# The low halves behind the first fused norm moved forward, the second variance behind the second fused norm moved back, and single idle products between the statistics products

## The reference, cut to what matters

```
def modulate(x, shift, scale):
    return layer_norm(x) * (1 + scale) + shift

def post_norm(x, y, gate, g, b):
    return layer_norm(ALPHA * x + gate * y) * g + b
...
        x = post_norm(x, mix_lat, g1, ln1_g[l], ln1_b[l])
        ffn_lat = conv_ffn(modulate(x, sh2, sc2), ffn_w_up[l], ffn_conv_w[l], ffn_conv_b[l], ffn_w_down[l], True)
        x = post_norm(x, ffn_lat, g2, ln2_g[l], ln2_b[l])
```

```
def hybrid_layer(h, p_i, cos, sin, g_mix, w_in, g_cq, w_q_up, w_iq_up, g_qn, g_kn, g_ik,
...
    xn = rms_norm(h, g_mix)
    proj = xn @ w_in
```

## Time and profile before

| | |
|---|---|
| Median of 3 runs | 2062.41 us (2062.07 to 2062.96) |
| The profiled execution's own time | 2063.26 us |
| Its span in the profile | 2061.5 us |
| TensorE busy | 2012.5 us, 98% |
| VectorE, GpSimd and ScalarE busy | 55%, 44%, 42% |
| p1, from the last sum to the first product that rests on it | 308.8 to 319.9 us |
| p2, the same | 693.0 to 700.6 us |

### The profile page before, as it was taken

The page is one execution under the profiler, slowest core; times in us unless marked ns, Lnnn a source line. Parts: engine busy times, 40 slices in busy tenths (PEclk is TensorE's granted clock), DMA queues, the critical chain, the costliest instruction groups (busy, mean ns, idle before and its releaser), DMA issues.

```text
span 2061.5 us, 26233 instructions
## 1 busy us (share of the span) xinstructions
PE 2012.5 (98%) x10138; PEld 1575.1 (76%) x10138; DVE 1136.5 (55%) x2020; ACT 867.5 (42%) x1381; POOL 916.4 (44%) x1157
## 2 busy tenths in 40 slices
PE   6999998999999999999999999999999999999998
PEld 3877676888888668668888888786776788888877
DVE  5366758988294579965522231466896543222235
ACT  4542434444232556784322222445578532222242
POOL 1344204867666325541555555302355155555540
PEclk9999999999999999999999999999999999999999
DMA  9034631332333211113333223222111333332331
GB/s 327 26 110 144 212 123 43 101 100 85 105 100 102 77 53 42 50 34 113 102 102 98 91 97 102 91 80 79 46 41 42 102 94 100 102 103 82 102 102 62
DMA packets 188299, 194.26 MB, mean 94 GB/s; under 512 B 8592, under 2 KB 184080, under 8 KB 187792
## 3 DMA queue, kind: packets, MB, share of 16 engines
q1 hardware_dynamic: 187600, 189.44, 28.5%
q10 hardware_dynamic: 576, 3.15, 0.4%
HBM read 190.48 MB, written 2.10 MB: 93 GB/s over the span
## 4 chain that ended last, share of the span: by engine, by line
PE 87%; DVE 7%; ACT 2%; POOL 2%; DMA 1%; issue 1%; SPq 0%; DVEq 0%; ACTq 0%; POOLq 0%
PE ps L808 20%; PE ps L809 20%; PE ps L810 20%; PE ps L827 3%; PE ps L829 3%; PE ps L828 3%; PE ps L855 2%; DVE mix L2505 1%; POOL wl L2895 1%; PE ps L844 1%; PE ps L845 1%; PE ps L846 1%; PE ps L1353 1%; PE ps L1426 1%; PE ps L1409 1%; PE ps L1372 1%
## 5 line engine op out<-in xcount | busy, mean ns | idle before, releaser
L2895 POOL TENSOR_TENSOR wl<-ring,wh 128x256 fp32r<-128x256 f32 x1008 | 753.9, 781 | 808.5 <-ACT wh L1463 808.4
L1463 ACT ACTIVATE wh<-ring 128x1024 fp32r<-128x1024 f32 (+1 forms) x298 | 309.0, 1044 | 313.6 <-PE ps L810 257.0
L808 PE MATMUL ps<-xh,wh 128*128 128x512 f32 (+1 forms) x976 | 383.8, 393 | 2.6 <-POOL wl L2895 2.6
L809 PE MATMUL ps<-xl,wh 128*128 128x512 f32 (+1 forms) x976 | 381.3, 391 | 0.0
L810 PE MATMUL ps<-xh,wl 128*128 128x512 f32 (+1 forms) x976 | 381.1, 391 | 0.0
L808 PE MATMUL ps<-acts,wh 128*128 128x512 f32 x880 | 343.5, 390 | 0.7 <-POOL wl L2895 0.4
L809 PE MATMUL ps<-acts,wh 128*128 128x512 f32 x880 | 342.4, 389 | 0.0
L810 PE MATMUL ps<-acts,wl 128*128 128x512 f32 x880 | 342.4, 389 | 0.0
L2505 DVE SCALAR_TENSOR_TENSOR mix<-ps,par,mix 128x441 f32<-128x441 f32 (+2 forms) x352 | 213.8, 693 | 32.6 <-ACT mix L1710 32.6
L808 PEld LDWEIGHTS ps<-xh,wh 128*128 128x128 f32 (+1 forms) x976 | 183.3, 188 | 47.6 <-issue 9.1
L810 PEld LDWEIGHTS ps<-xh,wl 128*128 128x128 f32 (+1 forms) x976 | 183.4, 188 | 39.2
(11 more groups left out here) (443 smaller groups left out, 3026.2 us busy)
## 6 DMA issues: line engine op xcount, KB each, us to landing
ring<-in_w_ff_dram SPq DMA_DIRECT2D x64, 1024.0 KB, 5.2
ring<-in_w_in_dram SPq DMA_DIRECT2D x28, 1024.0 KB, 5.0
ring<-in_ffn_w_up_dram SPq DMA_DIRECT2D x22, 1024.0 KB, 5.0
ring<-in_w_ada_dram SPq DMA_DIRECT2D x17, 1024.0 KB, 5.0
ring<-in_w_out_dram SPq DMA_DIRECT2D x12, 1024.0 KB, 5.1
ring<-in_ffn_w_down_dram SPq DMA_DIRECT2D x8, 1024.0 KB, 5.0
ring<-in_w_ple_gate_dram SPq DMA_DIRECT2D x8, 1024.0 KB, 5.0
early<-in_w_ada_dram SPq DMA_DIRECT2D x7, 1024.0 KB, 10.7
```

The source lines that it names most:

```text
L808: t.matmul(b[0:m, 0:n], s.hi[:, k, a:a + m], x2[0][:, k, :], start=k == ks[0], stop=False)
L809: t.matmul(b[0:m, 0:n], s.hi[:, k, a:a + m], x2[1][:, k, :], start=False, stop=False)
L1463: a.activation(s.hi[:, :, c], s.ap[:, :, c], ACT.Copy).then_inc(*up("hi", "hi", name, hf))
L2895: i = p.tensor_tensor(s.lo[:, k:k + 2, c], s.ap[:, k:k + 2, c], s.hi[:, k:k + 2, c].bitcast(F32), ALU.subtract)
```

## The change

It has three parts.

1. In p1's loop VectorE makes `xl` of row block j-1 behind the first of the three operations on row block j, where it stood behind the third. The number of operations stays the same. The wait of the second operation for the first is now for a named event, since another operation stands between.
2. In p2 the second variance (four small operations on VectorE), its root (ScalarE) and the reciprocal (VectorE) stood among the row blocks; they now stand behind the last one.
3. Five idle products are added: in p1 and in p2 one ahead of `tS` and one ahead of `dl`, and in p1 one ahead of `R2`. Each stands in front of the wait for its row, and goes into the bank that the row is then written to.

```
@@ statistics (TensorE)
                 b = take(("tS", tag), where=where[0])
+                spin(b, 1)
                 e.wait_ge(*taken(("parts", tag)))
...
-                spread(("dl", tag), st[:, :, 0], at("st", tag), where=where[1])
+                spread(("dl", tag), st[:, :, 0], at("st", tag), where=where[1], idle=1)
...
-            def spread(key, src, wait, keep=False, where=None):
+            def spread(key, src, wait, keep=False, where=None, idle=0):
 
                 b = take(key, keep, where)
+                spin(b, idle)
                 e.wait_ge(*wait)
...
-            spread(("R2", "p1"), inv2, at("r2", "p1"), keep=True)
+            spread(("R2", "p1"), inv2, at("r2", "p1"), keep=True, idle=1)
@@ p2 (ScalarE)
-                if j == 5:
-                    second_root("p2")
-
+
+            second_root("p2")
@@ p1 (VectorE)
+            def first_low(j):
+                e.wait_ge(*at("xh", "f", j))
+                v.scalar_tensor_tensor(xl[:, j, :], mix[:, j, :], mod3[:, 24 + j, 0:1], xh[:, j, :].bitcast(F32),
+                                       ALU.add, ALU.subtract).then_inc(*up("vec", "xl", "f", j))
...
-                    i.then_inc(*(up("vec") if j < 7 else free(("R1", "p1"))))
-                    e.wait_ge(*(now("vec") if j < 7 else taken(("R1", "p1"))))
+                    i.then_inc(*(up("vec", "step", j) if j < 7 else free(("R1", "p1"))))
+                    if j:
+                        first_low(j - 1)
+                    e.wait_ge(*(at("step", j) if j < 7 else taken(("R1", "p1"))))
...
-                if j:
-                    e.wait_ge(*at("xh", "f", j - 1))
-                    v.scalar_tensor_tensor(xl[:, j - 1, :], mix[:, j - 1, :], mod3[:, 24 + j - 1, 0:1], xh[:, j - 1, :].bitcast(F32),
-                                           ALU.add, ALU.subtract).then_inc(*up("vec", "xl", "f", j - 1))
+                if j == 8:
+                    first_low(7)
@@ p2 (VectorE)
-                if j == 5:
-                    second_variance("p2", False)
-                if j == 8:
-                    second_inverse("p2")
+            second_variance("p2", False)
+            second_inverse("p2")
```

## The result

The changed kernel has a median of 2058.74 us over 22 runs (2057.18 to 2061.03), the kernel before 2062.19 us over 22 (2059.31 to 2064.28, one execution of 2517.03 left aside). The ratio is 0.9986 with a 95% interval of 0.998 to 0.9992: 1.6 to 4.1 us faster, about 2.9. That is inside the 0.2% within which I had put it with 94%; the median itself lies 0.16 us under the lower end of the range. The forecast was -1.6 us.

The account below looks back on a forecast made before the run. TensorE, busy 98% of the span, was taken as the bound, with gains where it waits or runs slowly. -0.6 + 0.05 - 1.45 + 0.4 = -1.6 us gave a forecast of 2060.8 us, range 2058.9 to 2062.7.

Parts of the forecast that it names:

- -0.6 for the eighth row block: p1: TensorE begins the eighth row block (block 7) at 339.5 instead of 340.10, with one turn missed.
- a round of 2.98 us: p1: VectorE's low halves follow each other every 2.98 us in the new order, against 2.89 before.
- one turn missed: p1: a low half waits once for a GpSimd operation; -0.6 us. Rivals: two missed +0.6 (17%), none -1.6 (10%).
- near tie with GpSimd: p1: the first low half asks at 316.73, GpSimd begins at 316.75; it ends at 317.48 or, losing, 318.58.
- The loop through ScalarE: p1: the round runs from VectorE's third operation through ScalarE's `xh` to the low half and back, 2.98 us.
- Forecast -1.45: p2: without the four small operations among the row blocks, TensorE's wait of 1.45 us for a low half is gone.
- The cover of the 80-column weight's low half: p2: that low half is ready at 712.9, TensorE asks at 713.2; 0.25 us of cover.
- +0.4 in p2: p2: idle products stick out of the gaps ahead of `tS` and `dl` by 0.15 and 0.25 us; between 0 and 0.6.
- +0.05 in p1: p1: cost of the idle products, mostly covered by waits; ends 0 and +0.8, the latter if the clock stays at half.
- from the sum to the median: Whole kernel: -1.6 from the profiled 2063.26 gives 2061.7; the median, 0.85 lower at 2062.41, gives 2060.8.
- One stretch less behind p1's wait: Behind the wait ending at 345.12: a half-clock stretch worth 1.7 us goes, giving 2059.1; chance 8%.
- rival of one stretch more: p2's last four row blocks or first products after: another half-clock stretch costs 1.7 us, giving 2062.5; chance 9%.

Follow-up runs that it names:

- GpSimd cut short: The changed kernel with GpSimd's seven operations in p1 done on 8 of their 512 columns; one execution, 2056.06 us, for its trace alone.
- the third place: The changed kernel with p1's low half behind the second of the three operations instead of the first; 2057.69 us, ratio 0.999 to the kernel before.
- order and move: The changed kernel without its five idle products; 2057.28 us, ratio 0.9987 to the kernel before.
- 1.1 in the second: The changed kernel measured again beside the kernel before; 2058.67 us against 2061.23, ratio 0.9992.
- move alone: The kernel before with only p2's second variance, root and reciprocal moved behind the row blocks; 2059.72 us, ratio 0.999.
- The two shifts tried: The kernel before with one or two idle products ahead of the last of p1's eight output products; 2061.79 us (1.0004) and 2061.95 us (1.0005).
- idle products alone: The kernel before with only the five idle products added; 2062.68 us, ratio 1.0006.
- two of them ahead of p1: The kernel before with two idle products ahead of the last of p1's eight output products; 2061.95 us, ratio 1.0005.

## Why the prediction was right, and what it missed

*p1's order.* Forecast -0.6 for the eighth row block and a round of 2.98 us with one turn missed; measured -0.53 and 2.99, with one turn missed, by the first low half. The price of the near tie with GpSimd was right too (1.1 us, by the run with GpSimd cut short). The loop through ScalarE is shown by the third place: out of the loop, the row blocks are bound by TensorE from the fourth on (they begin 2.74 us apart in that profile, at 326.18 and 328.92).

*p2's move.* Forecast -1.45, measured -1.44. The cover of the 80-column weight's low half was forecast at 0.25 us and is 0.25.

*The idle products.* Forecast +0.4 in p2, measured +0.37; +0.05 in p1, measured 0.01. The +0.05 was weighed with a clock that stays at half, by which `R2` would come 0.8 us late. It did not: the clock was at its higher level (1.00) in p1 in all seven profiles with the idle products, and `R2`'s last transpose ended 5.67 us behind the last sum where it had ended 6.16 behind it. The Trainium skill, TensorE: Matmul & The Clock Gate, Part 4 (PE-mode transpose), says that a transpose does not count as TensorE being busy in the way other matmuls do. The traces agree, with an exception: with only `tS` and the transposes there the clock fell in p1 in six profiles of seven, and not in that of order and move. Nothing in p1 waits for it, so the idle products are a cost of 0.37 us and no gain.

*The sum.* -1.6 forecast, -1.5 by the parts and by the places of the changed kernel itself. **The step that failed** is the last one, from the sum to the median: "From the profiled execution's 2063.26 that is 2061.7; the median stands 0.85 lower". It carries the number of half-clock stretches of the kernel before over to the changed one. One stretch less behind p1's wait was my rival with 8%, and it is what the profile shows, with 1.5 of the 1.7 us that I gave it. My rival of one stretch more came true too, at 741.3 us, but at a place where it cost nothing and not 1.7 us. So the places were forecast rightly and for the right reasons, and the 2.1 us by which the median lies under 2060.8 come from the clock, a term that the sum had at nothing, or from chance (below). Over the runs the mean granted clock rose from about 0.9953 to 0.9973. Each stretch of 3.4 us at half takes 3.4 x 0.5 / 2060 = 0.0008 off the mean, so by this estimate there are some two and a half fewer of them. One to one and a half would be those in the norm pairs, which are free. The remaining one is worth about 1.5 us if it is the one behind p1's wait, which the means cannot tell: stretches near 741 and 1420 us are free as well. That would be the size of what the medians gained beyond the places: 3.45 - 1.5 = 1.9 us in the first comparison and 1.1 in the second, 1.4 by the first ratio but only 0.1 by the second. The kernel before itself had medians from 2061.2 to 2062.2 us in the four sets of runs, so up to 1.0 us of it can be the set.

*What stays open.* Why this one falls away in the changed kernel is not settled, nor that it does so in more executions than before. The idle products are not needed for it (the profiles of move alone and of order and move have no such stretch and none of them). The two shifts tried did not do it. What the profiles do show is how much comes from ahead of the change: p1's last sum ends at 305.9 to 306.4 us in the six executions whose first half-clock stretch comes early, and at 308.6 to 309.0 in the three that have a stretch at 267 us besides. With 11 runs of most kernels, a standard deviation of 0.8 to 1.9 us from run to run and one or two traces of each, the share that is chance can't be told from the share that is the change's.

## What to carry to other kernels

When a change is worth a microsecond in a kernel whose runs spread over five, measure it in the trace as a distance from the last common event ahead of it; these distances repeated within 0.05 us when medians of 11 runs could not tell the sign. Before moving an operation forward in a loop, add up the new loop through the other engine: one place earlier cost 0.1 us a round here, and one place later than that was worth 1.2 us more. In a stretch that is bound by another engine idle products are at best free (0.01 us in p1), and a cost where the chain behind them has no slack (0.37 us in p2). If they pay through the clock at all, then ahead of work that TensorE has ready and nothing else limits; the half-clock stretch there cost 1.5 us, but no run here shows that filling the wait gets it back.

## What the runs showed of the hardware beyond what was expected

- VectorE and GpSimd take turns, by whole operations, where both read two inputs in SBUF. A low half of 0.75 us that began within an operation of GpSimd ended 0.55 us behind that operation's end (319.25 and 319.80 in the kernel before). One that asked only 0.07 us before the end did not get the turn: in the changed kernel it asked at 315.34, GpSimd's next operation begins at 315.37 in the trace, and the low half ended 0.55 us behind the end of that one.
- Half the clock for 3.4 us in either norm pair cost nothing (p2's first row block at 7.57 us with and without it), and 1.5 us behind p1's wait, where TensorE is the bound. Another, at 1492.8 us in two profiles (idle products alone, and two of them ahead of p1), goes with 1.5 to 2.3 us more: from the 80-column product to the end these take 1348.6 and 1348.7 us, the other twelve 1346.4 to 1347.1.
- An idle product of two matmuls takes 0.9 us of TensorE (three of them 2.74 us), yet ahead of `tS` and `dl` in p2 only 0.37 us of two of them reached the end, the rest lying in waits that were there already.
